# Turning raw token rows and scaling them on the way out of PSUM, in a one-core hybrid decoder step

## What is computed

```python
x = x + token_mixers(rmsnorm(x, norm_mix_g), conv_buf, ...)   # 6 projections, a spatial gate, a depthwise conv of width 31
x = x + moe(rmsnorm(x, norm_ffn_g), ...)                      # top 4 of 32 experts, clamped SwiGLU
y = rmsnorm(x, norm_final_g)
# rmsnorm(x, g) = x * rsqrt(mean(x * x) + EPS) * g
# padded = [conv_buf (30 rows), glu];  conv state returned = the last 30 rows of padded
```

## Time and profile before

| | |
|---|---|
| median of 3 runs | 1290.15 us (1289.37 to 1290.32) |
| profiled execution, span from first to last instruction | 1288.5 us |
| around the span, median run minus span | 1.65 us |
| PE busy | 1174.2 us, 91% of the span |
| DVE busy | 605.2 us, 47% |
| ACT busy / POOL busy | 249.7 / 467.4 us |
| read from HBM | 447.0 MB, 349 GB/s over the span |

### The profile page before, as it was taken

One profiled execution on the slowest core, in us unless ns is written; L12 is line 12 of the kernel. 1 busy time (PEld: TensorE's weight loads), 2 busy tenths in 40 slices (PEclk: granted clock), 3 DMA queues, 4 the chain that ended last, 5 costly groups with the idle time before them and its releaser, 6 DMA issues.

```text
span 1288.5 us, 30593 instructions
## 1 busy us (share of the span) xinstructions
PE 1174.2 (91%) x11113; PEld 577.5 (45%) x11114; DVE 605.2 (47%) x1256; ACT 249.7 (19%) x487; POOL 467.4 (36%) x833
## 2 busy tenths in 40 slices
PE   8999999999999899798979998989989799899876
PEld 7777777775434333233323433433333233233232
DVE  2999983122644344354343442444524244444243
ACT  2012124001222122122212221212211122122112
POOL 1022300000444435445451454454444444535451
PEclk9999999999999999999989999999999999999997
DMA  9983442344899999999998799999999999999996
GB/s 260 337 269 119 144 135 105 129 155 166 334 385 399 421 421 422 421 421 421 422 421 364 307 398 422 420 422 421 422 421 421 421 421 421 422 421 408 421 421 254
DMA packets 94570, 448.97 MB, mean 348 GB/s; under 512 B 8526, under 2 KB 42894, under 8 KB 45339
## 3 DMA queue, kind: packets, MB, share of 16 engines
q1 hardware_dynamic: 93742, 446.55, 86.5%
q10 hardware_dynamic: 749, 1.19, 0.3%
q0 software_dynamic: 48, 0.85, 0.2%
HBM read 447.00 MB, written 2.42 MB: 349 GB/s over the span
## 4 chain that ended last, share of the span: by engine, by line
PE 55%; DMA 15%; DVE 13%; POOL 6%; issue 6%; SPq 3%; ACT 1%; DVEq 0%; POOLq 0%; ACTq 0%
PE banks L1369 20%; DMA ring<-in_w_down 15%; PE banks L1379 12%; DVE R L800 8%; PE banks L1164 8%; POOL ring L530 6%; PE banks L1086 4%; PE banks L1144 3%; PE banks L1123 2%; PE banks L1280 2%; SPq L398 1%; PE banks L1130 1%; PE banks L1153 1%; DVE R L809 1%; DVE R L812 0%
## 5 line engine op out<-in xcount | busy, mean ns | idle before, releaser
L1369 PE MATMUL banks<-ring,hT 128*32 128x512 f32 x3328 | 430.4, 611 | 62.3 <-POOL ring L530 57.5
L530 POOL COPY ring<-big 128x512 f32<-128x512 f32 x248 | 146.9, 641 | 554.4 <-SPq L404 554.4
L530 POOL COPY ring<-R 128x512 f32<-128x512 f32 x496 | 289.9, 631 | 113.4 <-DMA R<-in_w_up 113.4
L321 DVE TENSOR_TENSOR xt<-xt,banks 128x1024 f32<-128x1024 f32 x106 | 128.7, 1215 | 403.7 <-PE banks L1144 403.7
L1379 PE MATMUL banks<-ring,hT 128*32 128x256 f32 x3328 | 227.4, 392 | 18.4 <-DMA ring<-in_w_down 13.2
L1379 PEld LDWEIGHTS banks<-ring,hT 128*32 128x32 f32 x3328 | 107.5, 113 | 202.8 <-issue 123.3
L1164 PE MATMUL banks<-hT,ring 128*128 128x288 f32 x768 | 189.2, 407 | 0.2 <-ACT hT L554 0.2
L1369 PEld LDWEIGHTS banks<-ring,hT 128*32 128x32 f32 x3328 | 95.5, 111 | 195.6 <-POOL ring L530 81.1
L1164 PEld LDWEIGHTS banks<-hT,ring 128*128 128x128 f32 x768 | 145.7, 191 | 39.9 <-issue 0.3
L680 ACT COPY WT<-banks 128x256 f32<-128x256 f32 x52 | 19.4, 373 | 498.2 <-PE banks L1379 498.2
L800 DVE SCALAR_TENSOR_TENSOR R<-big,convw,R 128x256 f32<-128x256 f32 x240 | 108.1, 525 | 0.0
(11 more groups left out here) (252 smaller groups left out, 757.2 us busy)
## 6 DMA issues: line engine op xcount, KB each, us to landing
ring<-in_w_down SPq DMA_DIRECT2D x128, 1024.0 KB, 11.0
R<-in_w_up SPq DMA_DIRECT2D x124, 1024.0 KB, 18.1
ring<-in_w_up SPq DMA_DIRECT2D x70, 1024.0 KB, 9.4
big<-in_w_up SPq DMA_DIRECT2D x62, 1024.0 KB, 12.7
ring<-in_w_in SPq DMA_DIRECT2D x24, 1024.0 KB, 10.3
ring<-in_w_branch_b SPq DMA_DIRECT2D x4, 1024.0 KB, 4.9
ring<-in_w_branch_a SPq DMA_DIRECT2D x4, 1024.0 KB, 4.9
ring<-in_w_out SPq DMA_DIRECT2D x4, 1024.0 KB, 4.9
```

What stands on the lines that cost most here:

```text
L321: nc.vector.tensor_tensor(dst, dst, rows, ALU.add).then_inc(y_added, 1)
L530: ins = nc.gpsimd.tensor_copy(ring[:, k, h * 512:(h + 1) * 512], parked[k][:, h * 512:(h + 1) * 512])
L1369: ins = mm(UP[g * BLK:(g + 1) * BLK, :], xT[:, k, :], ring[:, k, g * 512:(g + 1) * 512], start=k == 0, stop=k == UP_SLOTS - 1)
```

## The change

Five edits:

- PE turns the raw rows `xt` and `xs_rows` as soon as they have landed, all 24 blocks in a row, and only then `vecrows`. The mean squares still come from ACT for token tiles 0 and 2, and for tile 1 from DVE (`bn_stats`). One root and one reciprocal serve all three. DVE writes the inverses on a diagonal (`inv_diag`), PE spreads them over all partitions with two matmuls against `ones`, ACT copies them to `inv_rows`, and DVE alone copies the eight channel tiles out of PSUM with gain and inverse in one instruction each.
- `conv_w` is loaded as 124 rows of 256 and turned as 2 blocks of 124 columns (before: 8 of 31).
- `b_up` is loaded as 128 rows of 512 and turned as 4 full blocks (before: 16 of 32).
- The new convolution states are turned by 16 matmuls against the identity whose outputs lie at partitions 0, 32, 64 and 96 of one bank. ACT copies that bank out in one instruction and issues 20 stores in place of 9.
- Waits follow: PE's first projection waits for `hT_ready`, SP for `x_transposed` and `squared`.

The core of the diff:

```diff
@@ scalar
-            for tt in range(NT):
+            for tt in (0, 2):
                 act.wait_ge(x_in[tt], 16)
...
-                act.wait_ge(squared, tt + 1)
-                root(ss[:, 4 + tt:5 + tt], ss[:, tt:tt + 1], 1.0 / D)
-
+            act.wait_ge(squared, 3)
+            root(ss[:, 4:7], ss[:, 0:3], 1.0)
+            act.wait_ge(inv_spread, 1)
+            nc.scalar.copy(inv_rows[:, 0:224], bank[0][:, T:512]).then_inc(inv_ready, 1)
+            nc.scalar.copy(inv_rows[:, 224:T], bank[1][:, T:T + T - 224]).then_inc(inv_ready, 1)
             act.wait_ge(evac_early, 1)
-            for c in range(0, KC, 2):
-                act.wait_ge(x_transposed, c + 1)
-                nc.scalar.mul(hT[:, c, :], bank[c][:, 0:T], col(NORM_MIX, c)).then_inc(hT_even, 1)
@@ scalar, c == 0
+                        act.wait_ge(st_transposed, 1)
+                        nc.scalar.copy(st_rows, bank[6][:, :].rearrange("p (s h d) -> p s h d", s=2, h=2)
+                                       ).then_inc(st_ready, 1)
+                        act.wait_ge(st_ready, 1)
+                        for j in range(QN):
...
+                            for t in range(DS):
...
@@ vector
+            dve.wait_ge(pe_early, 1)
+            V.tensor_copy(cols[:].rearrange("p v c -> p (v c)"), bank[7][:, 320:320 + 8 * KC]
+                          ).then_inc(evac_early, 1)
+            dve.wait_ge(rooted, 1)
+            link(V.reciprocal(ss[:, 4:7], ss[:, 4:7]))
             for tt in range(NT):
...
+                ins = V.tensor_scalar(inv_diag[:, token_slices(tt)], ident[:, 0:ROWS[tt]], ss[:, 4 + tt:5 + tt], None,
+                                      ALU.mult)
+            ins.then_inc(inv_turned, 1)
+            dve.wait_ge(evac_early, 1)
+            dve.wait_ge(inv_ready, 2)
+            dve.wait_ge(x_transposed, 1)
+            for c in range(KC):
+                V.scalar_tensor_tensor(hT[:, c, :], bank[c][:, 0:T], col(NORM_MIX, c), inv_rows, ALU.mult, ALU.mult
+                                       ).then_inc(hT_ready, 1)
@@ tensor
+            ins.then_inc(x_transposed, 1)
+            pe.wait_ge(vec_in, 16 * 8)
+            tr(bank[7][:, 320:320 + 8 * KC], vecrows[:]).then_inc(pe_early, 1)
+            pe.wait_ge(inv_turned, 1)
+            mm(bank[0][:, T:512], ones[:], inv_diag[:, 0:224], start=True, stop=True)
+            mm(bank[1][:, T:T + T - 224], ones[:], inv_diag[:, 224:T], start=True, stop=True).then_inc(inv_spread, 1)
@@ tensor, j == 0
-                    for c in range(KC):
-                        ins = tr(bank[2][:, c * W:(c + 1) * W], cw_rows[:, c * P:(c + 1) * P])
+                    for j in range(2):
+                        ins = tr(bank[2][:, j * QN * W:(j + 1) * QN * W], cw_rows[:, j * P:(j + 1) * P])
...
-                    for f in range(2 * KC):
-                        ins = tr(bank[3][:, f * NE:(f + 1) * NE], pairs[:, f // 2, f % 2])
+                    for f in range(4):
+                        ins = tr(bank[3][:, f * P:(f + 1) * P], pairs[:, f // 2, f % 2])
```

More of the change, by code:

```diff
@@ L722, in _ @@
             V.tensor_copy(same_row[:, 1:QN, :], same_row[:, 0:1, :].to_broadcast([P, QN - 1, NS])).then_inc(row_mask, 1)
-            for tt in range(NT):
-                if tt == 2:
-                    dve.wait_ge(pe_early, 1)
-                    V.tensor_copy(cols[:].rearrange("p v c -> p (v c)"), bank[7][:, 320:320 + 8 * KC]
-                                  ).then_inc(evac_early, 1)
-                r = ROWS[tt]
-                dve.wait_ge(rooted, tt + 1)
-                link(V.reciprocal(ss[:, 4 + tt:5 + tt], ss[:, 4 + tt:5 + tt]))
-                V.tensor_scalar(stage[0:r, tt, :], xs_rows if tt == 2 else xt[:, tt, :], ss[0:r, 4 + tt:5 + tt], None,
-                                ALU.mult).then_inc(xs_ready, 1)
-            for c in range(1, KC, 2):
-                dve.wait_ge(x_transposed, c + 1)
-                V.tensor_scalar(hT[:, c, :], bank[c][:, 0:T], col(NORM_MIX, c), None, ALU.mult).then_inc(hT_odd, 1)
+            dve.wait_ge(x_in[1], 16)
+            for h in range(2):
+                link(V.bn_stats(bnst[:, 1, h, :], xt[:, 1, h * 512:(h + 1) * 512]))
+            link(V.bn_aggr(mv[:, 1, :], bnst[:, 1, :, :]))
+            V.scalar_tensor_tensor(ss[:, 1:2], mv[:, 1, 0:1], mv[:, 1, 0:1], mv[:, 1, 1:2], ALU.mult, ALU.add
+                                   ).then_inc(squared, 1)
+            dve.wait_ge(pe_early, 1)
[3 more added lines that the diff above has]
+            link(V.reciprocal(ss[:, 4:7], ss[:, 4:7]))
+            for tt in range(NT):
+                ins = V.tensor_scalar(inv_diag[:, token_slices(tt)], ident[:, 0:ROWS[tt]], ss[:, 4 + tt:5 + tt], None,
[7 more added lines that the diff above has]
+                                       ).then_inc(hT_ready, 1)
             dve.wait_ge(history_turned, 1)
@@ L1091, in _ @@
             for tt in range(NT):
-                if tt == 1:
-                    pe.wait_ge(vec_in, 16 * 8)
-                    tr(bank[7][:, 320:320 + 8 * KC], vecrows[:]).then_inc(pe_early, 1)
                 r = ROWS[tt]
-                pe.wait_ge(xs_ready, tt + 1)
+                pe.wait_ge(x_in[tt], 16)
                 for c in range(KC):
-                    if tt == 1 and c == KC - 1:
-                        pe.wait_ge(evac_early, 1)
-                    ins = tr(bank[c][:, tt * P:tt * P + r], stage[0:r, tt, c * P:(c + 1) * P])
-                    if tt == 2:
-                        ins.then_inc(x_transposed, 1)
+                    rows = xs_rows if tt == 2 else xt[:, tt, :]
+                    ins = tr(bank[c][:, tt * P:tt * P + r], rows[:, c * P:(c + 1) * P])
+            ins.then_inc(x_transposed, 1)
[4 more added lines that the diff above has]
+            mm(bank[1][:, T:T + T - 224], ones[:], inv_diag[:, 224:T], start=True, stop=True).then_inc(inv_spread, 1)
             def keep_busy(n):
@@ L1220, in _ @@
                         for c2 in range(KC):
-                            if c2 == 4:
-                                pe.wait_ge(st_ready, 1) if q == 0 else pe.wait_ge(st_ready, 3)
-                            dst = bank[6 + q][0:(HIST, NS)[q], (c2 % 4) * P:(c2 % 4 + 1) * P]
-                            src = cprompt[:, c2, SEQ:SEQ + HIST] if q == 0 else glu_tail[:, c2, :]
-                            nc.tensor.transpose(dst, src, ident[:]).then_inc(st_transposed, 1)
+                            h, j = divmod(c2, QN)
+                            src = cprompt[:, c2, HIST + SEQ - NS:HIST + SEQ] if q == 0 else glu_tail[:, c2, :]
+                            ins = mm(bank[6][j * NS:(j + 1) * NS, (2 * q + h) * P:(2 * q + h + 1) * P], src, ident[:],
+                                     start=True, stop=True)
+                    ins.then_inc(st_transposed, 1)
                 if n == 2 * KC + 4:
```

64 lines of the change are left out of this document (31 added, 33 removed).

## The result

The changed kernel takes **1293.06 us** (median of 11 undisturbed runs, lowest 1291.98), the one before 1289.38 us (12 runs): ratio 1.003 with a 95% interval of 1.0021 to 1.0039. That is 2.7 to 5.0 us slower. One run of 1458 us at a granted clock of 0.75 is left out.

The account below looks back on a forecast made before the run. The prediction took DVE's column in the front as the bound: +2.65 (start) +1.7 (clock) -0.56 -0.15 (tables) = +3.6 us, a span of 1292.1 plus 1.65, so 1293.8 us; own range 1292.8 to 1294.8, overall 1290.4 to 1296.2.

Parts of the forecast that it names:

- The bound: Front, up to 193.95 us: DVE's column is 0.9 us longer than PE's, so delays to DVE's convolution delay the end.
- The start, +2.65 foreseen: Chain from `vecrows` to the first projection: projection starts 2.65 us later (2.1 to 3.3), near 14.5 instead of 11.87.
- two spread matmuls at 0.8: Start chain: PE's two matmuls spreading the inverses, 288 columns together, take 0.8 us (0.7 to 1.3 at the low clock).
- The clock, +1.7 foreseen: First projection: TensorE's clock is low for 3.4 us, costing half, 1.7 us (0 if no fall, 3.4 if twice as long).
- the low stretch of the tables: Earlier trace, about 31.7 to 35.1 us: TensorE at 1.2 GHz after small turned blocks; the pattern for 3.4 us low.
- the long rival: Projection: the low level carries over from the cold start and lasts twice as long, +5.3, 1295.5 us; chance 0.10.
- Tables, -0.71 foreseen: Taps, up bias and spatial matrices: DVE saves its 0.56 us wait, plus 0.15 on two copies (bounds -0.3 and +0.2).
- States, 0 foreseen: New convolution states: PE's savings don't count, since PE then waits longer at L1239; ACT's stores take 6.9 us for 3.1.
- the cover that was named: PE's wait for DVE at L1239 absorbs the states' savings; without it they would count up to 2.9 us.
- The join: L1239, PE's mean matmul after DVE's sum: PE's wait of 0.9 us grows to 4 to 6 us.
- The sum: End of DVE's column: +2.65 +1.7 -0.56 -0.15 = +3.6 us, giving a median of 1293.8 us; chance 0.50.
- a part swallowed: Expert stage: a rival had the experts' weight stream swallow the front's shift, 1290.2 us; chance 0.08.

Follow-up runs that it names:

- e8_delay_only: Kernel before plus 18 matmuls with unused results ahead of the last token tile, so only the start is later: 1293.82 us, ratio 1.0036.
- e2_tables_only: Kernel before with only the taps and up bias loaded and turned as wide tiles: 1289.21 us, ratio 0.9995.
- e3_states_only: Kernel before with only the convolution states turned by sixteen matmuls into one bank and 20 stores: 1290.97 us, ratio 1.001.
- e4_tables_states: Kernel before with the wide tables and the new states, but the old start: 1290.45 us, ratio 1.0003.
- e1_start_only: Changed kernel with tables and states as before, so only the new start remains: 1292.83 us, ratio 1.003 against the kernel before.
- e10_filler_again: Changed kernel plus four unused matmuls where PE waits in the start, measured a second time: 1291.43 us, ratio 1.0014 against the kernel before.
- e12_short_filled3: Changed kernel with two warm-up matmuls, `vecrows` earlier, one filler before the diagonal's wait and three after the spread: 1288.31 us, ratio 0.9992 against the kernel before.

## Why the prediction was right, and where its terms were off

**The bound.** That DVE's column, and not the nearly always busy PE, carries the front was the step on which all rested. It held: a delay of 4.75 us at the start reaches the loop as 4.7 (`e8_delay_only`), 0.8 us off DVE's tables arrive as 0.8 (`e2_tables_only`), and what PE alone saves is lost in the profiles of `e3_states_only` and `e4_tables_states`. That the medians of these two are 1.2 and 0.7 us above before is left without an explanation.

**The start, +2.65 foreseen.** It was +3.24 in one execution (at the upper end of 2.1 to 3.3) and +1.79 in the other (below the lower). The steps up to `cols` fell within 0.3 us (`vecrows` 10.98 for 11.3, the spread 12.41 for 12.55). What failed is one price: two spread matmuls at 0.8. They took 1.44 at the low clock (12.41 to 13.85) and 0.81 at the full one (11.60 to 12.41). The price was right for the full level, but I had no reason to take that level there, and even the bound that I gave for the low one, 1.3, was too small. In the second execution the chain came out shorter for another reason: the clock rose at 9.2, so the token blocks, priced at the low level, were done 1.0 us early (`vecrows` 10.26 for 11.3).

**The clock, +1.7 foreseen.** It cost 1.9 in the first course: the 64 records of the projection take 17.66 us, for 15.76 before, so the level was low from 15.11 to about 18.9. In the second it cost 2.9 (18.63 us for the records, low from 13.66 to 19.4). Chain and clock together were foreseen as 4.35 and measured as 5.1 and 4.7: DVE's copies of the old states start at 34.45 and 33.97, where the earlier trace rows have 29.30.

The forecast took the low stretch of the tables as its pattern: clock up, emptied by a gap, down for 3.4 us. In the first profile the low level was instead carried over from the cold start. That is the mechanism of the long rival, at less than its price. In the second profile the clock did rise and was emptied by gaps, as foreseen, but it stayed low for 6.8 us and not 3.4. So neither profile shows the foreseen course. In the second, a chain 0.9 too short and a clock 1.2 too dear nearly cancel, and that is luck. In the first profile the PEclk column doesn't show the low level. It reads 1.00 in both of these windows (PE and its records stand first):

```profile
18.00:19.00 1.00, 1.00 (x3) 0.67 (x2) 0.00 (x0) 0.00 (x0) 0.00 (x0) 1.00 1.16 273
19.00:20.00 1.00, 1.00 (x6) 0.77 (x5) 0.00 (x0) 0.00 (x0) 0.00 (x0) 1.00 1.12 316
```

Three projection records in one microsecond and six in the next: that is the rise, and the count of records is the gauge. Of the rule behind that rival (the Trainium skill, "TensorE: Matmul & The Clock Gate", Part 4: PE-mode transpose, by which turned blocks don't count as activity) the runs show that it can't be taken as absolute. Durations of the turned blocks in the second profile of the changed kernel, 6 to 9 us and from 9.2 us on:

```profile
L1097 PE MATMUL banks<-ident,xt x12: 421/421/454, 6.4 to 8.8; 128*128 128x128 f32 x12
...
L1097 PE MATMUL banks<-ident,xt x5: 272/283/421, 8.8 to 9.4; 128*128 128x128 f32 x5
```

Their time falls from 421 to 272 ns while PE does nothing but turn; its last other work, the warm-up matmuls, had ended by 6.6. In the first profile the same blocks stayed at 421 to the end. Why the same program does the one or the other stays open. The kernels that start as before show no such split: in all five profiles of them (before, `e2_tables_only`, `e3_states_only`, `e4_tables_states`, `e8_delay_only`) the 64 projection records take 15.76 us, the full level from the first. The mean clock of the span doesn't tell the courses apart, so I can't say from the runs without a profile how often each comes.

**Tables, -0.71 foreseen.** From the start of the state copies to the end of the spatial ones it is 4.81 us for 5.72: -0.91. The wait of 0.56 went, and the up bias copy in runs of four took 0.67 for 1.01, more than the -0.15 allowed for. The taps' single elements cost 0.58, for 0.40. But only a little of this belongs to the wide blocks: in `e1_start_only`, with narrow blocks and the clock kept up, the same stretch took 4.98 (33.98 to 38.96). Most of the gain is the low clock, and with it the wait, that the kernel before had there. PE kept its clock there in the profiles with wide blocks in the tables and lost it in that of before, in `e3_states_only` and in `e8_delay_only`, which have the narrow ones; `e1_start_only` has them too and kept it. So narrow blocks alone don't settle it.

**States, 0 foreseen.** Right in the profiles, through the cover that was named; the medians leave room for a cost, as said above. ACT's stores were dearer than 0.34 us. From the changed kernel's trace (durations, first and last start; then ACT's next two GELUs in the timeline):

```profile
L590 ACTq DMA_DIRECT2D out_conv_state_prompt<-R x4: 904/904/1027, 123.2 to 130.9; - x4
L594 ACTq DMA_DIRECT2D out_conv_state_sample<-R x16: 314/322/484, 124.3 to 133.0; - x16
...
133.42 0.71 ACT L582 ACTIVATE R<-banks 128x288 f32<-128x288 f32 x2 [10.26 <-issue]
```

The sample rows keep the price, the prompt's rows (a pattern over tokens and two halves) take 0.9 each. ACT is tied up for 10.2 us, between the 6.9 of the sum and the bound of 14. Its next GELU starts at 133.42. The later ones follow PE at 3.88 us each (138.26, 142.14, up to 149.90); counted back, this one's input was there by 126.6, so it comes about 6.8 us late, where about 1 was foreseen. The one after it comes 3.2 late and the third (134.38) on time. PE needed the bank only three outputs later, 11.6 us, and shows no wait for it.

**The join.** PE's wait was foreseen at L1239 with 4 to 6 us; it came with 3.1 us at the first mean matmul and none at the second. I had seen that PE gains on DVE, but not that the earlier of the two sums is where it runs into DVE first. Behind that wait the clock fell, which the forecast had priced only for the start. It cost PE 1.7 us and the end of this execution at most 0.2, because PE had them to spare.

**The sum.** Foreseen +3.6 for DVE's column. By the trace: 5.1 - 0.9 = +4.2 in the first profile, 4.7 - 0.9 = +3.8 in the second; the loop starts 4.2 and 3.7 later. The runs differ by 3.7 us. So the step that carried the forecast, a later start passed on by DVE's column, was right. That the sum agrees to 0.1 us with the runs is in part luck: the start and its clock were 0.3 to 0.8 dearer than priced, the tables gave 0.2 more, and the states may have cost something. The forecast of 1293.8 was 0.7 too high all the same, because its base was: the median of three runs, 1290.15, where twelve give 1289.38.

**What the loop seems to give back.** The shift is 4.2 at the loop's start and 2.6 at its end, and that looked like a part swallowed. But the loop of the profiled execution before lasted 910.4 us, and those of all fourteen profiles lie between 908.8 (changed) and 910.6 (`e10_filler_again`), with a mean of 909.55. The latest of them (`e8_delay_only`, 909.9) isn't shorter than the earlier ones (`e12_short_filled3`, 909.0). The fourteen spread over 1.8 us without any order by lateness, and two spans alone can't show a difference of that size.

## What to carry to other kernels

- Where two engines run in parallel, find at the join which one is waited for; every part of a change counts only as far as it moves that one, and savings of the other came back here as its wait. Check this on the medians too: one profile is one execution, and the profiles of `e3_states_only` and `e4_tables_states` were of executions 1.7 and 1.8 us below their medians. Here a clear loser (the start) and two parts with little or no effect stood in one change, and only separate kernels told that.
- Work that is begun early wins only if what had kept it from beginning is taken away too. Raw rows no longer needed the scaling, but the seven warm-up matmuls still held PE until 6.4 us; cutting them to two, with `vecrows` moved forward, turned a loss of 3.7 us into one of 0.4, which the runs can't tell from none, and fillers in the gaps made that a gain of 1.1 to 1.7, at the edge of what they can. And a normalisation moved behind the transposes becomes a chain of small steps over PE, DVE and ACT, with an idle PE in it.
- Price a matmul near an idle gap at both levels of the clock, and read the level from the count of records; fillers held the level in two kernels here, but at the low one they were a cost themselves.

## What the hardware showed that I had not expected

- The same program takes two courses in its first 20 us: TensorE reached its full level (2.4 GHz) at 9.2 in one execution and at about 18.9 in another, and the start of the projection moved by 1.45 us with it (13.66 and 15.11). With fillers the two courses stand 3.1 us apart at the loop, without them 0.5.
- After a wait of 1.07 us, 0.8 us of matmuls and part of a wait of 1.25, the clock stood at the low level (1.2 GHz) from 12.6 to 19.4, though PE had no gap from 13.66 on.
- A DMA issue on ACT's queue took 0.90 us for the prompt rows (two pieces of 128 elements from each row) and 0.32 for the sample rows. Before, the prompt rows went out whole in one issue of 0.36 us.
